# A transformer pair in fp32 on one core: 512-column products in the 27 token-shifted units of the second mixer, and the residual's scaling moved to the within-chunk stage

## The reference

```
x = rms_norm(h, final_g)                 # the residual that enters the second block
h = rms_norm(x, attn_norm_g)
proj = h @ w_in                          # 2048 -> 3072 + 288 shifted, then 1088 not shifted
prev = pad(proj)[:, :-1]
shifted = proj + (prev - proj) * mu      # for the r, k, v, w, a, g columns
y = concat(rwkv7(shifted), mla(rest))
x = x + y @ w_out                        # the normed residual is used again here
x = x + conv_glu_ffn(rms_norm(x, ffn_g))
```

## Time and profile before

| | |
|---|---|
| median of three runs | 2280.56 us (2279.8 to 2282.35) |
| the profiled execution: its time, its span | 2274.88 us, 2273.1 us |
| busy share of the span: PE, DVE, ACT, POOL | 98%, 74%, 47%, 24% |
| share of the chain that ended last: PE, DVE, issue, POOL, ACT, DMA | 85%, 5%, 3%, 2%, 2%, 2% |
| granted clock of PE, mean | 0.995 |
| the 27 shifted units | about 1000.9 to 1174 us of the span |
| the within-chunk stage | about 1292 to 1386 us of the span |

### The profile page before, as it was taken

How to read it: one execution, slowest core, us unless ns; L and a number is a source line. 1 busy time by engine, 2 the same in 40 slices (tenths; PEclk the granted TensorE clock), 3 DMA queues, 4 the chain that set the end, 5 groups by cost and what they waited for, 6 DMA issues and landing times.

```text
span 2273.1 us, 39333 instructions
## 1 busy us (share of the span) xinstructions
PE 2222.8 (98%) x14865; PEld 1968.8 (87%) x14865; DVE 1690.8 (74%) x2863; ACT 1068.1 (47%) x1427; POOL 553.8 (24%) x226
## 2 busy tenths in 40 slices
PE   7999999999999999999999999999999999999997
PEld 6888998888888988899999887888888888888886
DVE  7688668885888488888878655778888885447887
ACT  5444464444444554556545522444444443334444
POOL 4776631017667520210002302110000000000012
PEclk9999999999999999999999999999999999999999
DMA  7445345555545355554444300455555555555564
GB/s 256 158 179 178 140 167 186 185 185 186 181 164 179 131 184 185 185 200 165 153 165 174 93 2 20 148 185 185 185 185 189 189 191 187 185 185 187 187 218 166
DMA packets 69034, 384.93 MB, mean 169 GB/s; under 512 B 15088, under 2 KB 22768, under 8 KB 23984
## 3 DMA queue, kind: packets, MB, share of 16 engines
q1 hardware_dynamic: 68912, 383.22, 47.6%
HBM read 380.02 MB, written 3.18 MB: 169 GB/s over the span
## 4 chain that ended last, share of the span: by engine, by line
PE 85%; DVE 5%; issue 3%; POOL 2%; ACT 2%; DMA 2%; SPq 0%; POOLq 0%; DVEq 0%; ACTq 0%
PE ps L259 40%; PE ps L260 21%; PE ps L247 4%; PE ps L249 4%; PE ps L248 4%; PE ps L262 3%; DMA raw<-weights_dram 1%; PE ps L870 1%; POOL low L241 1%; POOL ssq L1130 1%; DVE low L234 1%; PE ps L851 1%; PE ps L1939 1%; DVE ps L709 1%; PE ps L859 1%
## 5 line engine op out<-in xcount | busy, mean ns | idle before, releaser
L259 PE MATMUL ps<-opA,whi 128*128 128x512 f32 x2340 | 828.4, 394 | 1.5 <-POOL low L241 1.5
L229 ACT ACTIVATE whi<-raw 128x2048 fp32r<-128x2048 f32 x346 | 660.2, 1909 | 87.3 <-DMA raw<-weights_dram 85.6
L260 PE MATMUL ps<-opA,low 128*128 128x256 f32 x2496 | 672.6, 279 | 0.2 <-DVE opA L987 0.2
L234 DVE TENSOR_TENSOR low<-raw,whi 128x2048 fp32r<-128x2048 f32 x252 | 577.3, 2291 | 65.2 <-ACT whi L229 49.6
L241 POOL TENSOR_TENSOR low<-raw,whi 128x2048 fp32r<-128x2048 f32 x95 | 436.5, 4607 | 444.0 <-ACT whi L229 417.5
L259 PEld LDWEIGHTS ps<-opA,whi 128*128 128x128 f32 x2340 | 438.7, 187 | 102.1 <-issue 2.5
L260 PEld LDWEIGHTS ps<-opA,low 128*128 128x128 f32 x2496 | 468.1, 188 | 13.7 <-DVE opA L987 0.5
L259 PE MATMUL ps<-opB,whi 128*128 128x512 f32 x1260 | 453.6, 399 | 17.6 <-DVE opB L408 11.7
L260 PE MATMUL ps<-opB,low 128*128 128x256 f32 x1344 | 364.5, 281 | 0.0
L268 ACT ACTIVATE crossed<-ps 128x256 f32<-128x256 f32 x168 | 64.5, 384 | 516.1 <-PE ps L262 515.9
L259 PEld LDWEIGHTS ps<-opB,whi 128*128 128x128 f32 x1260 | 238.5, 189 | 76.4 <-DVE low L402 10.5
(11 more groups left out here) (396 smaller groups left out, 2981.3 us busy)
## 6 DMA issues: line engine op xcount, KB each, us to landing
raw<-weights_dram SPq DMA_DIRECT2D x350, 1024.0 KB, 4.8
bias_t<-table_dram SPq DMA_DIRECT2D x16, 384.0 KB, 6.1
hT<-xT_dram SPq DMA_DIRECT2D x4, 512.0 KB, 9.0
out_dram<-hT SPq DMA_DIRECT2D x4, 512.0 KB, 2.9
lora_g<-lora_dram SPq DMA_DIRECT2D x1, 1024.0 KB, 5.0
p_in<-pT_dram SPq DMA_DIRECT2D x2, 256.0 KB, 2.7
lora_wa<-lora_dram SPq DMA_DIRECT2D x1, 512.0 KB, 5.4
chunk_mats_dram<-compact SPq DMA_DIRECT2D x4, 128.0 KB, 3.2
```

The source lines that it names most:

```text
L229: act.activation(whi[:, v % RING, :], raw[:, v % RING, :], ACT.Copy).then_inc(hi_done.sem, 1)
L234: v_.tensor_tensor(wlo(v % RING, 0, width), raw[:, v % RING, 0:width], whi[:, v % RING, 0:width].bitcast(F32), ALU.subtract).then_inc(lo_d ...
L259: pe.matmul(*cross, start=start, stop=False)
L260: mm = pe.matmul(ps[:, b, 0:T], wlo(s, w0, w0 + P), op[:, k, 0:T], start=False, stop=False)
```

## The change

In the 27 shifted units PE now multiplies by `both_halves`. ACT copies the right half of the bank into one of two buffers, `mix_cross` (`cross`, new), and DVE adds that copy to the left half in place, in the bank, ahead of L1432. DVE no longer waits for `mm_done` but for ACT's copy. One buffer and `rs1` lie where the first block's convolution weights lay, so that `rs1` is not overwritten later. The 16 `normed_h` leave `phase_mix`; the same instruction stands now in item n of the within-chunk stage for block n, between the mask of item n+1 and the wait for PE.

```diff
@@ names @@
-        rs1 = place("rs1", [P, T], at=area + 23 * T)
+        rs1 = par_of("conv_w", 1)
+        mix_cross = [par_of("conv_w", 0), place("mix_cross", [P, T], at=spare2 + 640)[:, :]]
@@ phase_mix @@
+            read = cross_read.ahead(SHIFTED)
@@ phase_mix, scalar @@
+                def cross(j):
+                    act.wait_ge(mm_done.sem, u0 + j + 1)
+                    if j >= 2:
+                        act.wait_ge(ev_done.sem, u0 + j - 2 + 3)
+                    act.activation(mix_cross[j % 2], ps[:, bank_of(j), T:2 * T], ACT.Copy).then_inc(read.sem, 1)
+
                 for j in range(IN2_UNITS):
                     act_split(act, u0, j)
                     n, part = (j - 3) // 3, (j - 3) % 3
...
+                    if j < SHIFTED:
+                        cross(j)
                     if j == 1:
@@ phase_mix, vector @@
-                def normed_h(c):
-                    v.scalar_tensor_tensor(hT[:, c, :], hT[:, c, :], par_of("final_g")[:, c:c + 1], rs1[:, :], ALU.mult, ALU.mult)
-
                 def shifted(j):
                     u, c = u0 + j, slot_block[j]
-                    v.wait_ge(mm_done.sem, u + 1)
+                    v.wait_ge(*read(j + 1))
+                    link(v.tensor_tensor(ps[:, bank_of(j), 0:T], ps[:, bank_of(j), 0:T], mix_cross[j % 2], ALU.add))
                     if j:
                         v.wait_ge(*mx["got"](j))
                     v.tensor_tensor(t0[:, 1:T + 1], ps[:, bank_of(j), 0:T], rs[:, :], ALU.mult).then_inc(mx["prev"].sem, 1)
@@ phase_mix, vector, after shifted(j) @@
-                    if 1 <= j < 4:
-                        for c in range(4 * j - 4, 4 * j):
-                            normed_h(c)
-                    elif j in (5, 8, 11, 14):
-                        normed_h(12 + (j - 5) // 3)
@@ phase_mix, tensor @@
-                    pe_unit(pe, u0, j, 0, op, ready=ready if j == 0 else None, bank=bank_of(j), free=j == 2, within=(6, root_sums) if j == 1 else None)
+                    pe_unit(pe, u0, j, 0, op, ready=ready if j == 0 else None, bank=bank_of(j), free=j == 2, wide=j < SHIFTED, within=(6, root_sums) if j == 1 else None)
@@ phase_within, vector @@
                     if n + 1 < len(items):
                         masked(v, n + 1)
+                    v.scalar_tensor_tensor(hT[:, n, :], hT[:, n, :], par_of("final_g")[:, n:n + 1], rs1, ALU.mult, ALU.mult)
                     v.wait_ge(*wi["ry"](n + 1))
                     v.tensor_tensor(r_[:, pair, t], ps[:, 5, 0:P], r_[:, pair, t], ALU.add)
```

## The result

| | before | after |
|---|---|---|
| median of the runs of the comparison | 2280.34 us (12 runs) | 2284.38 us (12 runs) |
| ratio, 95% interval | | 1.003 (1.0018 to 1.0041) |
| the profiled execution: time, span, mean granted clock | 2274.88, 2273.1, 0.995 | 2284.04, 2282.2, 0.992 |
| share of the chain: PE, DVE, issue | 85%, 5%, 3% | 83%, 6%, 4% |

The changed kernel is slower by 4.0 us in the medians (0.18%), and by 6.8 us in the middle of the ratio's interval, which goes from 4.1 to 9.3 us and leaves out no change. The forecast was 2283.4 us with "the same" (within 0.2%) as the likeliest reading. The time lies in its range, but the reading doesn't hold: the middle of the interval is 0.3%, on the slower side, which had 0.15. The question for the experiments is where 27 cheaper units lost more than they saved.

What follows compares the result with a forecast made beforehand. PE was taken as the bound. Savings of 4.05 us against losses of 1.43, 0.65 and 2.5 gave +0.5; the scaling's 2.3 made +2.8, added to the runs' median: 2283.4 us, range 2280.2 to 2285.6.

Steps and rivals of the forecast that it cites:

- the slower side: Whole kernel: the reading that the change makes it slower by over 0.2% (4.56 us); chance 0.15.
- What bounds the kernel, the products: Shifted units: PE is nearly always busy; 27 units with 512-column products save it 0.15 us each, 4.05 us.
- 1, the beginning: Unit 3's start: PE waits for DVE, which has two more sums, while PE comes 0.45 us earlier; price 1.43 us.
- 2, the logarithm behind the copy: Every third shifted unit: ACT's logarithm follows its copy, `rk` comes 3.7 us later and just meets PE; loss only 0.65 us.
- The third rival: Shifted units: the cycle through ACT becomes the period; each tenth of a microsecond over costs 1.0 us; chance 0.14.
- Behind unit 7: Shifted units: PE waits for `rk` because no small products L1643 have yet been run there; 0.65 us.
- 3, behind unit 26: End of the shifted units: DVE 2.0 us late, PE 0.45 early; PE's wait grows from 2.7 to 5.2, price 2.5 us.
- The scaling: Within-chunk stage: item 1's scaling waits for POOL's L241, making PE late for item 2; price 2.3 us.
- The sum: Whole kernel: +0.5 us in the shifted units and +2.3 in the within-chunk stage give +2.8 us.
- The profiled time as a base: Whole kernel: the profiled execution lies 5.7 us below the runs' median, so the forecast difference was added to the median.

Runs made afterwards that it cites:

- best: Changed kernel with copy behind logarithm, small products of pair 6 behind unit 27, reciprocal behind unit 29, scalings in items 4 to 15; 2268.54 us, ratio 0.9951.
- log_first: Changed kernel with ACT's copy of every third unit put behind the logarithm and exponentials; 2283.16 us, ratio 1.0008 to the kernel before.
- recip_late: Changed kernel with DVE's reciprocal of the second factor moved from unit 0 to behind unit 29; 2285.13 us, ratio 1.0021 to the kernel before.
- within_only: Kernel before with only the 16 scalings moved into the within-chunk stage, one in each item; 2284.18 us, ratio 1.0015.
- within_late: Kernel before with the 16 scalings moved into items 4 to 15 of the within-chunk stage, behind POOL's L241; 2280.71 us, ratio 1.0000.
- before_again: Kernel before, unaltered, profiled a second time; 2283.99 us in 1 run.
- after_again: Changed kernel, unaltered, profiled and timed again; 2287.12 us, ratio 1.0029 to the kernel before.
- mix_only: Changed kernel with the 16 scalings put back in the shifted units, leaving the 512-column products and two-step sum; 2281.95 us, ratio 1.0008 to the kernel before.

## Why the prediction was wrong

- *What bounds the kernel, the products.* Right. 4.05 us were there, and are there in full once nothing eats them (best, log_first).
- *1, the beginning.* +1.43 forecast; PE's wait went from 0.22 to 1.55 us, +1.33. That PE waits there for DVE's work on units 0 and 1 is shown by recip_late. The two sums are in the timeline with 0.46 us each (1007.49 to 1007.95, 1013.27 to 1013.73), 0.92 together; the rest is that PE comes earlier.
- *2, the logarithm behind the copy.* This step failed, in the sentence "It just meets: no loss in periods where L1643 lies between". The cycle was found and its links are there, but from the start of the copy to the end of `rk` it takes 1084.16 - 1071.38 = 12.78 us, where the count had 12.57 (1069.43 to 1082.0). The copy holds ACT for 0.40 us before the table load, counted with 0.31, and from DVE's low part to its sum it takes 2.32, counted with 2.20; why this one is longer than elsewhere no run shows. PE then starts its sums 0.14 behind the end of `rk`, for which the count had nothing. The way from one engine to the next was otherwise as counted: 0.44 us from the product to the copy (0.43), 1.93 from the split to the low part (1.94). In all, from the last product of unit 11 to the sums, 1084.30 - 1070.94 = 13.36 us and not 13.0. Where PE waits for nothing, it needs 1082.92 - 1069.79 = 13.13 for this (log_first). So PE stands 0.23 too long, and its sums take 0.75 until the next unit's first product where log_first has 0.68: together 0.30 us in each period, which is 19.67 - 19.37. log_first measures what this costs over the stage: 1.97 us. The third rival had this as a mechanism, with a chance of 0.14; its price, 1.0 us for each tenth, was too high: the sum below is off by 1.8 for 0.32. Behind unit 7 it was 0.81, forecast 0.65.
- *3, behind unit 26.* +2.5 forecast, +2.22 measured (2.69 to 4.91). The count there takes off 1.35 for a wait that its own sentence gives as 1.25.
- So the fixed part of the shifted units: -4.05 + 1.33 + 0.81 + 1.97 + 2.22 = +2.3, and 193.00 - 190.58 = +2.4 in the table. Forecast: +0.5.
- *The scaling.* Right in mechanism and size: 3.44 us for the instruction, 2.14 for the wait, forecast 2.3. within_only and within_late show both the cost and that the place makes it. The scaling ended behind POOL's first L241, as forecast.
- *The sum.* Fixed: 2.4 + 2.1 = +4.6 us, not +2.8; the missing 1.8 is the period of step 2. 4.6 is the 0.2% that the prediction took as the least that can be told apart, so this alone put it on the line.
- *A missing term.* The sum counts a wait of PE as its own length. In both profiles of after the clock was low behind the waits of 4.91 and 2.14, for 1.7 and 2.2 us in a, and 0.9 and 2.1 in C (14.31 and 15.52, less 11.24 + 2.14). All seven profiles with the wait of 2.13 or 2.14 us in item 2 lose 0.9 to 2.3 us there. In a, before pays it too, now and then (0 and 1.5 in its two profiles); in C it never did, having no wait there. Of the clock's part only C's is thus plainly the change's. How much more often the clock falls behind 4.9 us than behind 2.7 stays open: four profiles with 2.69 (before, before_again, within_only, within_late) lost 0, 1.5, 2.6 and 1.5 us in a, the five with 3.71 to 4.92 (after, after_again, mix_only, log_first, recip_late) 1.7, 2.2, 2.8, 2.6 and 2.3.
- *The profiled time as a base.* The 5.7 us between the profile of before and the median of the runs were added as a constant. They are mostly the clock's part, which this profile happened not to have: before_again's span is 9.1 us longer with the same fixed part of A.
- *Luck.* That 2284.38 came within 1 us of the forecast 2283.4 is in part luck. The fixed part was 1.8 us too low and the clock's part left out, and ten other runs of the same kernel (after_again) have a median of 2287.12, beyond the range's 2285.6.

## What to carry to other kernels

When an instruction is put ahead of the start of a serial chain that crosses three engines, and the count says that it just meets, treat that as a loss not yet found. Here three links were each 0.09 to 0.14 us longer than start-to-start distances from other places had them, no slack was left for it, and it was paid in every period. Put the new copy behind the chain's first link and ask again. A gain of less time on PE isn't had until the waits beside it are moved too; here four edits of order, none of which takes work away, turned a ratio of 1.0029 into 0.9951 (about +7 us into -11). One of the four alone, without the 512-column products, gives 4.8 of those 11 us: a control tells which part of a gain is the change's. And before two profiles are compared, take the same kernel twice: compare stretch by stretch, since stretches without a low clock repeat to 0.1 us where the spans differ by 9.

## What the runs showed of the hardware

- After PE has stood still for 2 to 5 us, its granted clock may fall to the lower level (1.2 GHz) for some microseconds. It did not with 2.69 us in one execution and did with 2.69 in another of the same kernel; over all such waits this cost 0 to 2.8 us each time for the same work. With 24 products put into the wait the clock was 1.00 in the one profile taken; since one of four profiles with 2.69 us of waiting had that too, it isn't shown that they did it.
- A scaling of 128 x 256 on DVE with both operands in SBUF took 0.47 us alone and 3.44 us beside POOL's L241 in item 1, and ended just behind it.
- POOL is held up too: beside the scaling of item 0 one of its short operations took 0.80 us, where its neighbours take 0.61, while the scaling took 0.96 instead of 0.47.
